# DeltaNet's second norm and the final norm by chunks, and an output in two transfers

## What is computed

```python
def rmsnorm(h, gain):
    y = hf * lax.rsqrt(jnp.mean(hf * hf, axis=-1, keepdims=True) + NORM_EPS)
    return (y * gain).astype(h.dtype)

def modulate(h, gain, shift, scale):
    return rmsnorm(h, gain) * (1.0 + scale) + shift

    # layer 1, the latents only
    hx = hx + mx[2] * yx                       # yx = delta_mixer(...), ends in  @ w_out
    hx = hx + mx[5] * peer(modulate(hx, norm2_g[i], mx[3], mx[4]), ...)
return rmsnorm(hx, final_g)
```

## Time and profile before

| | |
|---|---|
| median of three runs | 3529.57 us |
| the profiled execution's own time | 3527.6 us |
| its span, first to last instruction | 3525.8 us |
| mean granted TensorE clock | 0.954 of full speed |
| PE busy | 3290.8 us, 93% of the span |
| DVE busy | 2181.9 us, 62% |
| ACT busy | 1619.5 us, 46% |
| POOL busy | 158.8 us, 5% |
| read from memory | 522.42 MB, 150 GB/s over the span |

### The profile page before, as it was taken

How to read it: one execution, slowest core, us unless ns; L and a number is a source line. 1 busy time by engine, 2 the same in 40 slices (tenths; PEclk the granted TensorE clock), 3 DMA queues, 4 the chain that set the end, 5 groups by cost and what they waited for, 6 DMA issues and landing times.

```text
span 3525.8 us, 73154 instructions
## 1 busy us (share of the span) xinstructions
PE 3290.8 (93%) x25548; PEld 2881.3 (82%) x25548; DVE 2181.9 (62%) x4574; ACT 1619.5 (46%) x2856; POOL 158.8 (5%) x92
## 2 busy tenths in 40 slices
PE   8999999999999999999999997899889999579997
PEld 3799996588889999857888897877679999568886
DVE  1478856955556887496555662443348884885554
ACT  1344445754544444475445552222134444664543
POOL 0000000000000000000000463000000000000000
PEclk9999999999999999999999998998689999879999
DMA  6555554466564555444666441000045555026663
GB/s 252 174 184 184 167 184 149 130 194 195 191 211 164 180 181 173 162 144 155 218 192 206 147 143 49 3 2 2 24 143 173 184 168 183 30 74 195 202 194 108
DMA packets 143304, 530.25 MB, mean 150 GB/s; under 512 B 16528, under 2 KB 16672, under 8 KB 140768
## 3 DMA queue, kind: packets, MB, share of 16 engines
q1 hardware_dynamic: 140832, 512.96, 44.5%
q0 software_dynamic: 2368, 15.81, 1.2%
HBM read 522.42 MB, written 6.29 MB: 150 GB/s over the span
## 4 chain that ended last, share of the span: by engine, by line
PE 77%; DVE 11%; issue 7%; POOL 2%; ACT 1%; DVEq 1%; DMA 0%; SPq 0%; ACTq 0%; POOLq 0%
PE pS L1593 11%; PE pS L1595 11%; PE pS L1594 11%; PE pY L1722 10%; PE pY L1724 10%; PE pY L1726 10%; PE pY L1777 4%; PE pS L1777 3%; PE pS L1513 2%; POOL lo L1465 2%; PE pG L1777 2%; DVE buf L1069 2%; DVE raw L1057 2%; DVE gated L1062 1%; DVE raw L1062 1%
## 5 line engine op out<-in xcount | busy, mean ns | idle before, releaser
L942 DVE TENSOR_TENSOR lo<-raw,hi 128x1024 fp32r<-128x1024 f32 x824 | 1009.2, 1225 | 789.6 <-ACT hi L527 785.7
L527 ACT CAST hi<-raw 128x1024 fp32r<-128x1024 f32 x872 | 913.6, 1048 | 538.0 <-PE pY L1726 507.5
L1593 PE MATMUL pS<-h_hi,hi 128*128 128x256 f32 x3584 | 1021.8, 285 | 34.9 <-DVE h_lo L1165 21.4
L1594 PE MATMUL pS<-h_lo,hi 128*128 128x256 f32 x3584 | 1017.3, 284 | 0.0
L1595 PE MATMUL pS<-h_hi,lo 128*128 128x256 f32 x3584 | 1017.2, 284 | 0.0
L1593 PEld LDWEIGHTS pS<-h_hi,hi 128*128 128x128 f32 x3584 | 691.3, 193 | 42.1 <-issue 38.8
L1594 PEld LDWEIGHTS pS<-h_lo,hi 128*128 128x128 f32 x3584 | 691.4, 193 | 0.1
L1595 PEld LDWEIGHTS pS<-h_hi,lo 128*128 128x128 f32 x3584 | 691.2, 193 | 0.0
L1722 PE MATMUL pY<-hi,h_hi 128*128 128x512 f32 x1536 | 474.6, 390 | 7.2 <-DVE h_lo L1093 7.2
L1724 PE MATMUL pY<-lo,h_hi 128*128 128x512 f32 x1536 | 474.4, 390 | 0.0
L1726 PE MATMUL pY<-hi,h_lo 128*128 128x512 f32 x1536 | 474.2, 390 | 0.0
(11 more groups left out here) (285 smaller groups left out, 3237.5 us busy)
## 6 DMA issues: line engine op xcount, KB each, us to landing
raw<-in_blocks SPq DMA_DIRECT2D x872, 512.0 KB, 3.4
gate_mod<-in_mod_wT SPq DMA_DIRECT2D x56, 512.0 KB, 3.5
raw<-in_mod_wT SPq DMA_DIRECT2D x20, 512.0 KB, 4.6
buf<-in_mod_wT SPq DMA_DIRECT2D x20, 512.0 KB, 6.4
buf<-in_keysT POOLq DMA_DIRECT2D x3, 1024.0 KB, 5.2
buf<-in_window SPq DMA_DIRECT2D x2, 1024.0 KB, 13.6
spill_x_res<-buf POOLq DMA_DIRECT2D x2, 1024.0 KB, 4.9
spill_x_h<-buf POOLq DMA_DIRECT2D x2, 1024.0 KB, 6.8
```

Source lines behind the costliest of these rows:

```text
L527: s.copy(hi[slot][:, :, :], raw[slot][:, :, :]).then_inc(hi_ready, 1)
L942: v.tensor_tensor(lo[slot][:, :, :], raw[slot][:, :, :], hi[slot][:, :, :].bitcast(F32), ALU.subtract).then_inc(lo_ready, 1)
L1593: t_.matmul(out, hi[slot][:, c, :], h_hi[:, c, :], start=(c == 0), stop=False)
L1594: t_.matmul(out, hi[slot][:, c, :], h_lo[:, c, :], start=False, stop=False)
```

## The change

It has two parts.

In the W_OUT loop, the eight blocks are written out on PE, ACT and DVE. Each residual add signals `y_res` by itself; ACT squares that chunk and DVE multiplies it by the norm's gain and scale (into `hn`), one block later; PE sums the chunk's squares two blocks later, between two blocks. Behind the last block PE has the sums of chunks 5, 6 and 7 left. The product with the reciprocal then gives `nrm` without the shift, in two halves; ACT adds the shift as it casts `h_hi` (Identity with a bias, chunk by chunk) and DVE as it forms `h_lo` (three operands). POOL's write of `res[0]` waits for `y_res` and no more for the norm.

At the end PE signals `y_chan` after every four transposes. DVE adds two chunks at a time, ACT squares them, PE sums them. DVE multiplies by the final gain ahead of the reciprocal, and the last product comes in two halves, each of which SP writes out.

```diff
@@ sync @@
             stream_peer(2, K2, L1)
+            for f in range(2):
+                sp.wait_ge(normed, 9 + f)
+                sp.dma_start(out[:, 4 * f:4 * f + 4, :], nrm[:, 4 * f:4 * f + 4, :]).then_inc(out_done, 16)
+            sp.wait_ge(out_done, 32)
@@ scalar @@
-            with act.Fori(0, NC // RING) as n:
-                for j in range(RING):
-                    split_hi(n, KD + NKV + NIN, j + AHEAD)
-            norm(6, res[0], lambda: act.wait_ge(y_res, NC))
-            act.wait_ge(normed, 7)
-            h_high(nrm)
+            def square(c0, c1):
+                s.activation(sq[:, c0:c1, :], res[0][:, c0:c1, :], ACT.Square).then_inc(squares, 1)
+
+            for j in range(NC):
+                split_hi(None, KD + NKV + NIN, j + AHEAD)
+                if j:
+                    act.wait_ge(y_res, j)
+                    square(j - 1, j)
+            act.wait_ge(y_res, NC)
+            square(NC - 1, NC)
+            norm_root(6)
+            for f in range(2):
+                act.wait_ge(normed, 6 + f + 1)
+                for c in range(4 * f, 4 * f + 4):
+                    i = s.activation(h_hi[:, c, :], nrm[:, c, :], ACT.Identity, bias=mods[:, 1, 3 * NC + c, 0:1])
+                i.then_inc(h_hi_ready, 1)
             peer(2, K2, E3, True)
-            act.wait_ge(fin_ready, 3)
-            norm(7, res[0], lambda: None)
+            for q in range(4):
+                act.wait_ge(fin_ready, 3 + q)
+                square(2 * q, 2 * q + 2)
+            norm_root(7)
@@ vector @@
-            with ve.Fori(0, NC // RING) as n:
-                for j in range(RING):
...
-            ve.wait_ge(evacuated, E3 + 2)
-            v.memset(mark[:, 6:7], 0.0).then_inc(y_res, NC)
-            norm(6, res[0], 1, 1, 0)
-            h_low(5, nrm)
+            def scaled(c):
+                ve.wait_ge(y_res, c + 1)
+                return v.tensor_scalar(hn[:, c, :], res[0][:, c, :], mods[:, 1, 4 * NC + c, 0:1], None, ALU.mult)
+
+            for j in range(NC):
+                split_lo(None, KD + NKV + NIN, j + AHEAD)
+                ve.wait_ge(block_done, KD + NKV + NIN + j + 1 + RING)
+                x = res[0][:, j, :]
+                v.scalar_tensor_tensor(x, pS[j % 2][:, 0:T], gate1[:, j:j + 1], x, ALU.mult, ALU.add).then_inc(evacuated, 1)
+                ve.wait_ge(evacuated, E3 - NC + 2 + j + 1)
+                v.memset(mark[:, 6:7], 0.0).then_inc(y_res, 1)
+                if j:
+                    scaled(j - 1)
+            link(scaled(NC - 1))
+            ve.wait_ge(std_ready, 7)
+            link(v.reciprocal(inv_std, std))
+            for f in range(2):
+                c = slice(4 * f, 4 * f + 4)
+                v.tensor_tensor(nrm[:, c, :], hn[:, c, :], inv_std.unsqueeze(1).to_broadcast([P, 4, T]), ALU.mult).then_inc(normed, 1)
+            for f in range(2):
+                ve.wait_ge(h_hi_ready, 2 * 5 + f + 1)
+                for c in range(4 * f, 4 * f + 4):
+                    ins = v.scalar_tensor_tensor(h_lo[:, c, :], nrm[:, c, :], mods[:, 1, 3 * NC + c, 0:1], h_hi[:, c, :].bitcast(F32),
+                                                 ALU.add, ALU.subtract)
+            ins.then_inc(h_split, 1)
             peer(2, K2, E3, True)
-            ve.wait_ge(y_chan, 3)
             ve.wait_ge(res_in, 48)
-            add_branch(4, res[0], y_chunk, 1, 5, 0, fin_ready)
-
+            for q in range(4):
+                ve.wait_ge(y_chan, 3 + q)
+                for c in (2 * q, 2 * q + 1):
+                    i = v.scalar_tensor_tensor(res[0][:, c, :], y_chunk(c), mods[:, 1, 5 * NC + c, 0:1], res[0][:, c, :], ALU.mult, ALU.add)
+                i.then_inc(fin_ready, 1)
+            ve.wait_ge(fin_ready, 6)
+            link(v.tensor_tensor(hn, res[0], fin_g2[:, :].unsqueeze(2).to_broadcast([P, NC, T]), ALU.mult))
             ve.wait_ge(std_ready, 8)
             link(v.reciprocal(inv_std, std))
-            link(v.tensor_tensor(hn, res[0], inv_std.unsqueeze(1).to_broadcast([P, NC, T]), ALU.mult))
-            v.tensor_tensor(nrm, hn, fin_g2[:, :].unsqueeze(2).to_broadcast([P, NC, T]), ALU.mult).then_inc(normed, 1)
+            for f in range(2):
+                c = slice(4 * f, 4 * f + 4)
+                v.tensor_tensor(nrm[:, c, :], hn[:, c, :], inv_std.unsqueeze(1).to_broadcast([P, 4, T]), ALU.mult).then_inc(normed, 1)
@@ gpsimd @@
-            pool.wait_ge(normed, 7)
+            pool.wait_ge(y_res, NC)
             pool.dma_start(a["x_res"], res[0]).then_inc(spilled, 16)
...
-            pool.wait_ge(normed, 8)
-            pool.dma_start(out, nrm).then_inc(out_done, 16)
-            pool.wait_ge(out_done, 16)
@@ tensor @@
-                mm.then_inc(y_chan, 1)
+                    if g == 2 and c % 2:
+                        mm.then_inc(y_chan, 1)
+                if g < 2:
+                    mm.then_inc(y_chan, 1)
...
-            s_blocks(KD + NKV + NIN, E3 - NC, NC)
-            norm(6)
+            def square_sum(count, c):
+                pe.wait_ge(squares, count)
+                return t_.matmul(pG[0][:, 0:T], ones_mean, sq[:, c, :], start=(c == 0), stop=(c == NC - 1), skip_group_check=True)
+
+            for j in range(NC):
+                s_block(None, KD + NKV + NIN, E3 - NC, j, pS[j % 2][:, 0:T], 2)
+                if j >= 2:
+                    square_sum(6 + j - 1, j - 2)
+            for c in (NC - 2, NC - 1):
+                mm = square_sum(6 + c + 1, c)
+            mm.then_inc(mean_sq, 1)
             peer(2, K2, E3, True)
-            norm(7)
+            for c in range(NC):
+                mm = square_sum(6 + NC + c // 2 + 1, c)
+            mm.then_inc(mean_sq, 1)
```

More of the change, by code:

```diff
@@ L497, in preload @@
             def preload(func):
-                s.activation(table[:, tables[0]:tables[0] + 1], eps[:, :], func)
+                s.activation(table[:, tables[0] % 10:tables[0] % 10 + 1], eps[:, :], func)
                 tables[0] += 1
@@ L515, in norm_root @@
                 if k == 2 or k > 3:
-                    act.wait_ge(normed, k if k > 3 else 1)
+                    act.wait_ge(normed, (1, None, k, k, k, 8)[k - 2])
                 s.activation(norm_std[k] if k < 4 else std_c if k == 4 else std, pG[1 if k < 3 else 0][:, 0:T], ACT.Sqrt,
@@ L1589, in s_block @@
                 slot = (k0 + j) % RING
-                pe.wait_ge(lo_ready, RING * n + (k0 + j + 1 + RING))
-                pe.wait_ge(evacuated, RING * n + (e0 + j + 3 - banks))
+                pe.wait_ge(lo_ready, RING * n + (k0 + j + 1 + RING) if n is not None else k0 + j + 1 + RING)
+                pe.wait_ge(evacuated, RING * n + (e0 + j + 3 - banks) if n is not None else e0 + j + 3 - banks)
                 for c in range(NC):
```

## The result

The changed kernel takes 3506.66 us (median of 6 runs, 3500.55 to 3509.87), the kernel before 3529.82 beside it (6 runs, 3525.39 to 3530.53). The ratio is 0.9935, 95% interval 0.9922 to 0.9948, so 18.4 to 27.5 us faster; the medians lie 23.2 us apart.

The account below looks back on a forecast made before the run. PE was taken to bound the W_OUT loop, chains of single operations the norm behind it and the end. Terms +3.0 - 8.0 - 9.35 - 0.7 = -15.05 us gave 3514.5 us, range 3507 to 3523.

Parts of the forecast that it names:

- the store: Output write at the end: two SP halves land sooner than POOL's one, 0.7 us won (bounds none to 2.0).
- the 1 us for the spread of stages that the change leaves alone: Forecast range: its lower end was widened by 1 us for the runs' own spread.
- The loop, 3.0 us lost: W_OUT loop: five chunk sums between blocks delay PE by 0.60 us each, 3.0 lost (bounds 2.15 to 4.0).
- The norm, 8.0 won: Norm behind DeltaNet: last residual add to PE's next block takes 11.24 us instead of 19.21, 8.0 won.
- The end up to the last issue, 9.35 won: Kernel's end: second store issued at 3510.15 where POOL's was at 3519.50, 9.35 us won.
- The gate stage, -4.1 to +7.1: Last gate stage: its time depends on where the half clock falls, -4.1 to +7.1 us, not set by the change.
- The starting point: Whole kernel: profiled execution took 3527.6 us, and the median of three runs lies 2.0 above it.
- the loop did not eat the gain: Rival, W_OUT loop: new waits make PE stand about 1 us in each of seven blocks, 3520.5; 8 in 100.
- the table switches did not cost more than their loads: Rival, norm and end: each of two exposed ACT table switches takes another 1.3 us, 3517.1; 5 in 100.
- written-out code did not starve PE: Slower rival, W_OUT loop: eight written-out blocks each wait on instruction issue, 25.6 us in all, 3540.1; 3 in 100.
- the sums of five chunks do stand between the blocks: Rival, W_OUT loop: sums stay behind everything and only the end's reordering pays, 3522 or so; 4 in 100.
- the whole gate stage at half clock: Rival, last gate stage: all of it runs at half clock, 3521.6; 1 in 10.

Follow-up runs that it names:

- sp_store: The kernel before with its one 1024 KB output store issued by SP instead of POOL; 3525.04 us against 3526.14, ratio 0.9994.
- pool_out: The changed kernel with both output stores issued by POOL instead of SP; 3507.93 us, ratio 0.9952 to the kernel before.

## Why the forecast was wrong, by its own steps

The sign and the chains were right, the sum was 15.05 where the stages show 18.3 and the medians 21 to 23. The step of the sum that failed is the store; the step of the range that failed is the 1 us for the spread of stages that the change leaves alone. By steps:

- **The loop, 3.0 us lost: mis-sized.** I gave each of five chunks 0.60 and had 0.43 as the lower bound. It was the bound: the loop takes 27.9 us instead of 25.9. The last pass's 0.38 is the length of a record, not a step, and the next block's matmuls start inside it. 1.0 us too pessimistic.
- **The norm, 8.0 won: right.** 11.24 forecast, 11.34 measured, every term within 0.15. The table load in the open cost 1.30, as the row of DeltaNet's norm said. The Trainium skill's 2.66 us for a switch ("ScalarE: Activation LUTs", What ACT_TABLE_LOAD costs) is not borne out here: from the Square's end to the Sqrt's start are 1.31 us (2566.33 to 2567.64).
- **The end up to the last issue, 9.35 won: right.** The second store was issued 10.11 us behind the first residual add, 10.2 forecast, and that stage shrank by 9.3 to 9.6. That the last passes would run at the full clock was left open in the sum; they did, and the Sqrt waited 0.16 us for them.
- **The store, 0.7 won: this step failed.** I took "what follows the landing stays" and only priced the landing. What was won behind the last issue was 3.1: the landing went from 4.1 to 2.8, and what follows it from 2.2 to 0.4, because SP, not POOL, is the last to wait (`sp_store` and `pool_out`). The term is 2.4 us off, the largest miss in the sum, and outside the bound of 2.0 that I had set.
- **The gate stage, -4.1 to +7.1: the mechanism right.** It swings by 4.4 us between executions, at 0.1 us per us of half clock, inside these bounds. No run shows that the change sets it; that it does not is not shown either (56 us against 68 at the half clock, on average).
- **The starting point.** Three runs of the kernel before gave 3529.57; in later comparisons its median was 3527.54, 3526.14 and 3524.41. The stages ahead of the W_OUT loop alone differ by 10 us between profiles, and I had put 1 us into the range for them. With the two mis-sized terms right, 3.4 us together, the forecast would have been 3511, still inside the range; what carried the time below 3507 are the 4.9 us by which the medians' 23.2 exceed the stages' 18.3. Over three profiles each, the mean spans are 20.2 us apart (3523.3 and 3503.1): 18.6 in the four touched stages, 0.4 in the queries, 0.9 ahead of them all and 0.3 in gate stage and V together.

The rivals: the loop did not eat the gain; the table switches did not cost more than their loads; written-out code did not starve PE; the sums of five chunks do stand between the blocks; the whole gate stage at half clock did not come (at most 87 us of 131.6, in `sp_store`). What stays open: why the clock falls in the gate stage at one time and not at another, and whether the change has a part in it, what POOL does behind the landing, and the last 1 to 3 us between the profiles' 20.2 and the medians' 21.1 and 23.2, which lie within their intervals.

## What to carry to other kernels

Cut a kernel's last stages into pieces, and try an engine that only issues transfers, here SP, for issuing and awaiting the last store. Such a change is judged by the end of the span, so price what follows the landing as well as the landing. Price work laid between back-to-back matmuls by the distance of starts, not by the length of records. When a stage set by DVE runs at times at the half clock, try to fill PE's waits there with matmuls of no use, and look at whether they end before DVE lets PE go on. And before a forecast's range is drawn, take two or three profiles of the same kernel: they tell how far its untouched stages lie apart.

## What the runs showed that I had not expected

- Who awaits the last store matters more than how it is cut: behind the landing 2.2 us with POOL and 0.4 with SP, for one transfer of 1024 KB and for two of 512 KB alike.
- Sixteen matmuls of no use per octet made the kernel 4.7 to 7.3 us faster, with a granted clock of 0.95 over the gate stage, and 1.00 in the windows shown, where it was 0.67 to 0.82 over the stage without them.
- Forty of them, 4.0 us, in PE's wait for the split brought PE's first matmuls behind it to 0.38 and 0.28 us, from 0.58 and 0.41, worth 1.9 us in the stage that follows.
- Summing five chunks between the blocks, as the change does, costs some 2.0 us in the loop and saves 1.1 in the norm. By these two stages all eight sums behind the loop are 0.7 to 1.0 us better; the timings can't tell.
